# Seven quarter products for the gate and up pairs of three feed-forward stages

## The reference, cut to what matters

```python
def swiglu(h, w_gu, w_down):
    gate, up = jnp.split(h @ w_gu, 2, axis=-1)
    return (jax.nn.silu(gate) * up) @ w_down

h = h + 0.5 * m[2] * swiglu(modulate(rms_norm(h, norm_ffn1[l]), m[0], m[1]), ffn1_w_gu[l], ffn1_w_down[l])
...
h = h + 0.5 * m[8] * swiglu(modulate(rms_norm(h, norm_ffn2[l]), m[6], m[7]), ffn2_w_gu[l], ffn2_w_down[l])
```

## Time and profile before

| | us |
|---|---|
| median of 3 runs | 3365.09 |
| lowest, highest | 3362.91, 3369.96 |
| the profiled execution's own time | 3367.02 |
| its span, first to last instruction | 3365.3 |
| mean granted TensorE clock | 0.985 |

### The profile page before, as it was taken

The page is one execution under the profiler, slowest core; times in us unless marked ns, Lnnn a source line. Parts: engine busy times, 40 slices in busy tenths (PEclk is TensorE's granted clock), DMA queues, the critical chain, the costliest instruction groups (busy, mean ns, idle before and its releaser), DMA issues. The chain is left out here.

```text
span 3365.3 us, 67083 instructions
## 1 busy us (share of the span) xinstructions
PE 3231.2 (96%) x28066; PEld 2765.1 (82%) x28066; DVE 1817.0 (54%) x2677; ACT 1157.8 (34%) x1839; POOL 439.7 (13%) x312
## 2 busy tenths in 40 slices
PE   6999999999988999999999999999999989899998
PEld 5888888886667878888888888888886668789897
DVE  4552554565667655543554553454555766655353
ACT  3331222225665333321222431222224654344231
POOL 2000001000705310000002000001100616120000
PEclk9999999999999999999999999999999999999999
DMA  5231221342000012222221222222232000122222
GB/s 201 91 109 66 94 96 60 127 156 89 1 17 3 4 57 81 93 98 77 90 90 57 94 98 71 81 93 85 85 141 110 2 18 3 34 88 94 90 91 94
DMA packets 68270, 263.34 MB, mean 78 GB/s; under 512 B 7552, under 2 KB 8704, under 8 KB 67456
## 3 DMA queue, kind: packets, MB, share of 16 engines
q1 hardware_dynamic: 67664, 256.95, 22.1%
q10 hardware_dynamic: 432, 3.88, 0.3%
HBM read 258.70 MB, written 2.10 MB: 77 GB/s over the span
## 5 line engine op out<-in xcount | busy, mean ns | idle before, releaser
L240 PE MATMUL ps<-hn_hi,w_hi 128*128 128x512 f32 (+1 forms) x3520 | 864.8, 327 | 17.9 <-DVE hn_lo L457 5.9
L240 PE MATMUL ps<-hn_hi,w_lo 128*128 128x512 f32 (+1 forms) x3520 | 865.4, 327 | 0.0
L240 PE MATMUL ps<-hn_lo,w_hi 128*128 128x512 f32 (+1 forms) x3520 | 861.1, 326 | 0.0
L217 ACT ACTIVATE w_hi<-raw 128x1024 fp32r<-128x1024 f32 (+1 forms) x300 | 338.5, 1128 | 1375.4 <-PE ps L240 1217.7
L222 DVE TENSOR_TENSOR w_lo<-raw,w_hi 128x1024 fp32r<-128x1024 f32 (+1 forms) x300 | 396.9, 1323 | 469.5 <-ACT w_hi L217 462.0
L240 PEld LDWEIGHTS ps<-hn_hi,w_hi 128*128 128x128 f32 x3520 | 547.9, 190 | 82.3 <-issue 17.6
L240 PEld LDWEIGHTS ps<-hn_lo,w_hi 128*128 128x128 f32 x3520 | 548.3, 190 | 58.3
L240 PEld LDWEIGHTS ps<-hn_hi,w_lo 128*128 128x128 f32 x3520 | 545.2, 190 | 58.1
L240 PE MATMUL ps<-g_hi,w_hi 128*128 128x512 f32 (+1 forms) x1424 | 398.0, 347 | 6.1 <-DVE g_lo L894 6.1
L240 PE MATMUL ps<-g_lo,w_hi 128*128 128x512 f32 (+1 forms) x1424 | 403.5, 351 | 0.0
L240 PE MATMUL ps<-g_hi,w_lo 128*128 128x512 f32 (+1 forms) x1424 | 397.5, 347 | 0.0
(11 more groups left out here) (274 smaller groups left out, 3795.8 us busy)
## 6 DMA issues: line engine op xcount, KB each, us to landing
raw<-wgu SPq DMA_DIRECT2D x176, 512.0 KB, 3.4
w_mod_one<-wmod SPq DMA_DIRECT2D x100, 512.0 KB, 3.3
raw<-wdn SPq DMA_DIRECT2D x64, 704.0 KB, 4.1
raw<-win SPq DMA_DIRECT2D x44, 512.0 KB, 4.5
w_mod_two<-wmod SPq DMA_DIRECT2D x28, 512.0 KB, 3.6
w_mod_first<-wmod_first SPq DMA_DIRECT2D x4, 2048.0 KB, 23.2
raw<-wout SPq DMA_DIRECT2D x16, 512.0 KB, 3.3
h<-xT ACTq DMA_DIRECT2D x1, 3072.0 KB, 9.8
```

What stands on the lines that cost most here:

```text
L217: act.activation(w_hi[s][:, 0:kt, :].rearrange("p k n -> p (k n)"), raw[s][:, 0:kt * P], ACT.Copy).then_inc(hi_ready[s].sem, 1)
L240: mm = pe.matmul(out[:, o:o + b - a], w[:, k, :], m[:, k, a:b], start=(k == 0 and w is w_hi[s] and m is mov_hi), stop=(k == kt - 1 and w i ...
```

## The change

Three of the four feed-forward stages (those with 768 tokens) go through a new function `ffn_seven`. The last keeps `ffn`.

The 22 pairs are taken in groups of 4, 2, 4, 4, 4, 4; each group's down products come right behind its pairs and are added to `h`, so there are 48 additions instead of 16. The down weights are laid out to match, two row tiles (or four) in one 128 x 1024 block.

The first group's four pairs are computed as before, with gate and up products of 48 matmuls. Beside them the input is normed into `x_norm` and cut into quarters: the tokens in halves of 384 (and two shift columns), the contraction in halves of 4 tiles. Sums and differences of the quarters are made and split into hi and lo parts (`normed`, `first_sum` to `fourth_sum`, `moving_hi`, `moving_lo`).

The other 18 pairs are the 2 x 2 block product of (gate, up) x (contraction halves) by (contraction halves) x (token halves), done with seven products in place of eight: each has 4 contraction tiles x 3 parts = 12 matmuls of 386 columns. VectorE makes four weight sums per pair (`weight_sum`) and the low parts of five quarter weights (`slot_lo_made`) and one whole block (`gate_lo_made`), ScalarE their high parts; ScalarE copies product 0 out of PSUM, and VectorE combines the others with seven additions.

In the first group two modulation rows are made per pair; one more comes in the eighth pair, and five beside the down products of each of groups 2, 3 and 4. At the end of a stage ScalarE squares the tiles of `h`, and GpSimd only adds. All loops are written out.

The diff, cut to what decides the order:

```diff
+            mods_of = {n: (2 * n, 2 * n + 1) for n in range(PLAIN)}
+            mods_of[FIRST[2] + 1] = (8,)
+            mods_of.update({("down", j): tuple(range(5 * j - 1, 5 * j + 4)) for j in (2, 3, 4)})
...
+                @block.sync
+                def _(sp):
...
+                    for j, z in enumerate(SIZES):
+                        for n in range(FIRST[j], FIRST[j] + z):
+                            mods = mods_of.get(n, ())
+                            gate_raw_free(n)
+                            load(0, DOWN[j, 0] if last_of(n) else A["wgu"][l, which, 2 * n + 2])
+                            for m in mods[:1]:
+                                load_mod(m)
+                            up_raw_free(n)
+                            load(1, DOWN[j, 1] if last_of(n) else A["wgu"][l, which, 2 * n + 3])
+                            for m in mods[1:]:
+                                load_mod(m)
+                        if z == 4:
+                            lo_there(sp, j, "01")
+                            load(0, DOWN[j, 2])
+                            lo_there(sp, j, "2")
+                            lo_there(sp, j, "3")
+                            load(1, DOWN[j, 3])
...
+                        for m in mods[:1]:
+                            load_mod(m)
+                        for s, src in enumerate(srcs):
+                            for unit in freed_by[s]:
+                                lo_there(sp, j, unit)
+                            load(s, src)
+                            for m in mods[1:] if s == 0 else ():
+                                load_mod(m)
...
+                @block.gpsimd
+                def _(pool):
+                    for t in range(1, KD - 1):
+                        pool.wait_ge(h_squared.sem, h_squared.at(t))
+                        pool.wait_ge(sq_summed.sem, sq_summed.at(t))
+                        pool.tensor_tensor(sum_sq[:, 0:NT], sum_sq[:, 0:NT], h_sq[:, :], ALU.add).then_inc(sq_summed.sem, 1)
...
+                            act.activation(h_sq[:, :] if t else sum_sq[:, 0:NT], h[:, t, :],
+                                           ACT.Square).then_inc((h_squared if t else sq_summed).sem, 1)
...
+                    def way_down(j):
+                        z, n = SIZES[j], FIRST[j] + SIZES[j]
+                        mods = mods_of.get(("down", j), ())
+                        for unit in ("3", "4", "5") if z == 4 else ():
+                            down_lo_made(dve, j, unit)
...
+                        for m in mods[:1]:
+                            mod_product(m)
+                        for t in range(KD):
+                            if j < LAST and t == 7:
+                                (slot_lo_made if z == 4 else weight_sum)(dve, 5 if z == 4 else 4, n)
+                            add_down(j, t)
+                            if j == 0 and t == 1:
+                                quarter_lo(1)
+                            if z == 4 and t == 1:
+                                down_lo_made(dve, j, "6")
+                            if j < LAST and t == (2 if z == 4 else 0):
+                                gate_lo_made(n)
+                            for m in mods[1 + t:2 + t]:
+                                mod_product(m)
...
+                            if z == 4 and t == 3:
+                                down_lo_made(dve, j, "7")
...
+                            if j == LAST and t:
+                                gained_lo(dve, t - 1, nxt[3], hn_hi_ready.at(KD + 1 + t + 1), nxt[4])
...
+                    for n in range(PLAIN):
+                        mods = mods_of[n]
+                        scaled(n, 0)
+                        if not last_of(n):
+                            gate_lo_made(n + 1)
+                        else:
+                            two_tiles_lo(0)
+                        if n == 0:
+                            normed("B11")
+                        elif n == 1:
+                            first_sum()
+                        elif n == 2:
+                            moving_lo(2, t1, 2)
...
+                        mod_product(mods[0])
+                        if last_of(n):
+                            mod_product(mods[1])
+                        scaled(n, 1)
+                        if not last_of(n):
+                            up_lo_made(n + 1)
...
+                        for n in range(FIRST[j], FIRST[j] + z):
+                            gate_first(n)
+                            if not last_of(n):
+                                gate_lo_made(n + 1)
+                                weight_sum(dve, 2, n + 1)
+                            elif z == 4:
+                                two_tiles_lo(j)
+                            with_sixth(n)
+                            with_fifth(n)
...
+                            for k in range(LP):
...
+                                for w, m in ((slot_hi[p], M_OF[p][0]), (slot_hi[p], M_OF[p][1]), (slot_lo[p], M_OF[p][0])):
+                                    mm = pe.matmul(bank(n, p), w[:, k, :], m[:, k, 0:HW],
+                                                   start=(k == 0 and w is slot_hi[p] and m is M_OF[p][0]),
+                                                   stop=(k == LP - 1 and w is slot_lo[p]))
...
+                        together = 2 if z == 4 else 4
+                        for t in range(together):
+                            down(j, t, range(z - 1))
+                        for t in range(together):
+                            down(j, t, (z - 1,))
+                        for t in range(together, KD):
+                            down(j, t, range(z))
...
-            ffn(l, 0, NT, [A["win"][l, s] for s in range(2)], (0, MOD_FIRST) if first else (l, 3 * KD), fresh=first,
-                nxt=(l, "nm", 3, NT, True))
+            ffn_seven(l, 0, [A["win"][l, s] for s in range(2)], (0, MOD_FIRST) if first else (l, 3 * KD), first,
+                      (l, "nm", 3, NT, True))
```

667 lines of the change are left out of this document (660 added, 7 removed).

## The result

| | before | after |
|---|---|---|
| median, us | 3366.16 (3359.96 to 3370.62, 14 runs) | 3371.95 (3364.6 to 3378.84, 14 runs) |
| profiled execution, own time | 3367.02 | 3370.19 |
| its span | 3365.3 | 3368.4 |
| granted clock, mean | 0.985 | 0.971 |

The ratio is 1.0018, interval 1.001 to 1.0027. The forecast was 3335, and its range ended at 3362.

The account below looks back on a forecast made before the run. TensorE, busy for 96% of the span, was taken as the bound. 3367.0 - 125.7 (matmuls) + 44 (tile 7) + 14 (first group) + 3 (stage ends) + 29 + 4 (clock) = 3335 us; bounds 3300 to 3358, range up to 3362.

Parts of the forecast that it names:

- The tile-7 stalls: Eighth down tile of groups 2, 3 and 4: TensorE waits 4.9 us for VectorE's low part, nine times, +44 us.
- The walk: Step-by-step timing of VectorE's queue and the loads; it had part "7" ready at 34.5 us, wanted at 29.7.
- T: The end of a group's last gate/up product, from which the times in the down phase are counted.
- The bound of 58: Tile-7 stalls in all, in place of 44 us, if the first modulation load takes 1.6 us more.
- The 386-column cadence: Seven-product pairs: 174.2 ns per matmul, 14.63 us a pair, 54 pairs giving -125.7 us (-114 at 176.7 ns).
- The first group: Down tile 1 waits for the up product's scaling, 5.2 us, 3.8 in the first stage: +14 us for three.
- The stage's end: The low part of tile 6 follows VectorE's last addition, 1.1 us more: +3 us for three stages.
- The clock: TensorE restarts at 1.2 GHz behind twelve new stalls, 2.4 us each: +29 us; half for three stage ends: +4.
- (a): Rival: down phases are covered, no modulation row holds up tile 7; 3244 us, to 3300; chance 0.27.
- (b): Rival: VectorE bounds the seven-product pairs at 15.8 us each; 3399 us; chance 0.12 together with (c).
- (c): Rival: the 386-column stream runs by its weight loads, 0.2265 us each; 3570 us; chance 0.12 together with (b).
- stalls longer than walked but below (b): Outcome between the forecast's bounds and (b), 3358 to 3374 us; chance 0.06.

Follow-up runs that it names:

- lo7: The changed kernel with the low part of down tile 7 made ahead of the fifth modulation row instead of behind it: 3315.63 us, ratio to before 0.9852.
- rows_kept: The changed kernel loading only the first nine modulation rows of a stage, with VectorE's work on later rows kept (outputs not the reference's): 3285.48 us.
- first: The changed kernel with the second modulation row of pair 3 made behind the low part of the ring, not ahead of the up product's scaling: 3349.42 us.
- squares: The changed kernel with the squares of the residual at the stage's end given back to GpSimd: 3379.65 us, ratio 1.0055.
- placed: The kernel before with only the changed kernel's memory layout (normed-input row 772 for 784 columns, weight regions 5664 for 5632 bytes apart): 3358.66 us, 0.9982.
- narrow: The kernel before with only the row of the normed input 772 in place of 784 columns wide: 3355.07 us, ratio 0.9971.
- spaced: The kernel both with the weight regions 5632 bytes apart in place of 5664: 3259.22 us, ratio 0.969.
- both: The changed kernel with lo7's and first's moves, and a group's first modulation row loaded ahead of the down weights: 3271.28 us, ratio 0.9719.
- align: The changed kernel with each weight region 32 bytes longer (spacing 5696), so that all start at multiples of 64 bytes: 3365.76 us.
- small_adds: The kernel both with GpSimd's six additions of squares at each stage's end cut to one column (outputs not the reference's): 3260.33 us.

## Why the prediction was wrong, step by step

The mechanism was right in its main parts, and the sign was wrong because the sizes of the losses were: the net of -32 was a small difference of 126 us of gain and 94 of loss. The difference to the profiled execution's own time is 3370.2 - 3335 = 35 us. The two traces give, for the three changed stages (clock: what TensorE's busy time lost by the lower level, summed from the granted clock):

| us, after less before | forecast | measured |
|---|---|---|
| TensorE's work, at full speed | -125.7 | -115.5 |
| TensorE idle | +61 | +86.4 |
| lower clock, behind the first and the third stage's ends too | +33 | +32.4 |
| the rest of the kernel | 0 | -0.2 |
| sum | -31.7 | +3.1 |

By term:

- **The tile-7 stalls, forecast 44, measured 63.5 (+19.5): the step that failed most.** The place, the cause and the count were right, and lo7 and rows_kept showed cause and remedy. The walk had the first row used up at T + 11.2; it was T + 12.0 on average (1500.48 + 2.4 - 1490.9 in the rows above), since the first load, behind a weight load, took 4.6 us to land. The round was taken as 5.65 us and took 6.03, the mean of 36. Four rounds are 1.5 us longer, and the first came 0.8 late. The 5.65 came from a wait of 3.27 us in the kernel before; here the buffer stays empty for 3.4 to 4.0 us. Other loads are not the reason: in the phase shown SyncE issues nothing but four row loads before the stall is over.

```profile
1502.88 18.76 SPq L280 DMA_DIRECT2D w_mod_one<-wmod  x4
1528.01 0.33 SPq L960 DMA_DIRECT2D raw<-wgu  x1
```

The loads themselves are slower in this kernel, from issue to landing, against the earlier trace rows:

```profile
DMA to landing us min/median/max: 3.3/3.6/5.8
```

The bound of 58 in the text covered a late first load only, and the range did not add the bounds up.
- **The 386-column cadence, forecast 14.63 us a pair, measured 14.87 (+13).** The choice between 174.2 and 176.7 ns was the wrong one: "one size" was the reason given, and the pure stream is no cheaper than the mixed one. The mixed rows of the same mean width, were the nearer row. (The line gives 174.1, too; the sum was off by 0.1 ns.) Some 3 us came back, since the stages' other matmuls ran a little faster than before.
- **The first group, 14 against 12.8 (-1).** Right, with its mechanism: first removed exactly these three waits.
- **The stage's end, forecast 3.** Measured idle 12.2 against 5.1 before, so 7.1 (+4). The sum took 1.1 us for the low part where its own had 2.88 us beside GpSimd; the bound of 5 was the value to take, since the additions are still there. "GpSimd keeps only its adding" hid this, and "costs nothing" for the squares was wrong on the good side: squares showed 8 to 13 us.
- **Small waits** for the ring and for the next group's PSUM bank, 2.0 us in five places and 0.9 elsewhere: counted as nothing (+3).
- **The clock, forecast 29 for twelve restarts and 4 for the stages' ends, measured 32.4 in all (-1).** All fifteen restarts were followed by the lower level, the three ends too, where the forecast had half of them; each cost 2.2 us rather than 2.4.
- **The rest of the kernel, forecast 0, measured 0.** Inside it the last stage's own matmuls take 3.3 us longer, as they do in placed by the weight regions' spacing, and the other stages as much less. That the layout made placed 6.6 us faster doesn't carry over: its gain lies in the mixed pairs, of which the changed kernel has 12 left of 66.

Together 19.5 + 13 - 3 - 1 + 4 + 3 - 1 is 34.5 of the 35.

**The rivals.** (a) did not happen, but its kernel exists: with the three moves of order it took 3271, which is the 3244 of (a) plus 10.8 us of matmul work (the cadence), 3.2 more idle time at the stage ends, 7.0 of small waits and 6.2 of clock. (b) did not: VectorE's own pace is 13.47 us a pair. One pair a stage, the one that makes the ninth modulation row too, takes VectorE 15.8 us, and the pairs behind it make up for that. (c) did not, 177 ns against 226. The result, 3372, fell into the gap that the text had named "stalls longer than walked but below (b)", with 0.06: by its own bounds (cadence 11, loads 14, end 5) the forecast reached 3365, so that case was priced too low.

What the text said would show it did: 9 and 3 waits in the places named, the lower clock behind them (0.50 to 0.72 over the next 5 us), and VectorE's waits for modulation loads (45 + 3, where some 36 were named).

## What to carry to other kernels

Where an instruction that another engine needs is queued behind a chain of load and use through one buffer, every round's error adds to one stall, and the stall is paid again in clock. Put the needed instruction ahead of the chain, issue the first load before the loads that wait, and only then count the work saved. Where a forecast is the small difference of large terms, add their bounds up before giving a sign.

## What the runs showed of the hardware

- **GpSimd slows VectorE's two-input reads of memory.** Beside a 768-column addition of GpSimd of 1.8 to 1.95 us, a low part of 0.69 us takes 1.92, one of 1.22 takes 2.02, one of 1.14 takes 2.5 to 2.7. In the rows above, the low part starts at 1834.43 and GpSimd is done at 1835.96: waiting for it all would be 1.53 + 1.13 = 2.66 us, and 2.47 is measured. The Trainium skill, "SBUF — State Buffer", section "SBUF: two separate sides", says that a VectorE operation with two SBUF inputs and a GpSimd operation that reads SBUF hold a shared pair of ports exclusively and for a whole instruction, so that the other blocks; the trace agrees to 0.2 us.
- **TensorE's pace depends on where operands lie.** 512 columns: 7.48 us for 33 matmuls with weight regions 5632 bytes apart (before, narrow, spaced) and 7.65 with 5664 or 5696 (placed, both, align), an effect of 2%. The moving rows 772 in place of 784 columns wide, with the regions behind them 768 bytes lower: 0.6% on the mixed streams, 8.7 us of the whole kernel, more than the change itself moved it.
- **The pace is not a line in the columns:** 120.8 ns at 258, 175.4 at 384, 176.8 at 386, 226.5 at 512. The Trainium skill, "TensorE: Matmul & The Clock Gate", section "Back-to-back issue gap", has N / 2.4 + 2.5 ns for the gap of a matmul by itself, an estimated 163.3 at 386; the trace, a stream with a weight load for every matmul, has 13 ns more.
- **Idle time and the clock.** The clock did not go by the length of one idle time alone. At the starts of stages and at the groups' down tiles, over the traces of all kernels, TensorE ran on at granted 1.00 behind each of 41 idle times of 1.48 to 1.77 us. From 1.81 to 2.71 us it went either way: in lo7 the nine waits at tile 7 were followed by 1.00 five times (1.58, 1.63, 1.68, 1.81 and 2.15 us) and by 0.66 or 0.67 over the next 5 us four times (1.82, 1.90, 2.04 and 2.19 us); behind 2.71 us (small_adds) it was 0.66, 0.50 and 1.00. Behind each of 95 idle times of 3.31 us and more the clock fell, to 0.50 to 0.72 over the next 5 us. In the mixing part, where TensorE is idle more often, it also fell behind 1.25 us (before). In spaced, behind 3.58 us, the first pair of matmuls still ran at full speed (0.59 us) and the fall came behind it. So the cut in lo7 brought some of the clock back too: behind the nine waits 6.8 us were lost to the lower level, 19.0 in the changed kernel.
- **The same load takes longer in the kernels with written-out stages.** 128 x 1024 float32 from issue to landing, medians of 100 loads: 3.23 to 3.26 us in the three kernels with the old stages (before, placed, narrow) and 3.60 to 3.69 in the 13 others that make all 100 loads. Weight loads in the last stage, whose code is the same in all, show it too: 3.19 to 3.22 against 3.52 to 3.62. By placed it isn't the layout; what it is was not found. It is 0.4 us in each round of a chain of load and use.
